# Feed-forward entries of a streaming encoder: six pairs of weight chunks as seven block products each, with the block sums made on GpSimd

## What is computed

```python
def pre_mod(h, g_pre, shift, scale):
    return rmsnorm(h, g_pre) * (1 + scale[:, None, :]) + shift[:, None, :]
def swiglu(x, w1, w2):
    g, u = jnp.split(x @ w1, 2, axis=-1)
    return (jax.nn.silu(g) * u) @ w2
...
for l in range(DEPTH):
    mp = adaln(c_prompt, w_ada[l], b_ada[l])
    ...
    hp = post_add(hp, swiglu(pre_mod(hp, g[0], mp[0], mp[1]), ffn_w1[l, 0], ffn_w2[l, 0]), g[1], mp[2], FFN_RES)
    ...
    hp = post_add(hp, swiglu(pre_mod(hp, g[4], mp[6], mp[7]), ffn_w1[l, 1], ffn_w2[l, 1]), g[5], mp[8], FFN_RES)
```

## Time and profile before

| | |
|---|---|
| median of 3 runs | 2681.08 us |
| the profiled execution | 2681.71 us, span 2679.8 us |
| PE, PEld busy | 2645.8, 2563.3 us |
| DVE, ACT, POOL busy | 1636.2, 963.1, 200.0 us |
| matmuls | 20698 |
| granted PE clock, mean | 0.997 |

### The profile page before, as it was taken

How to read it: one execution, slowest core, us unless ns; L and a number is a source line. 1 busy time by engine, 2 the same in 40 slices (tenths; PEclk the granted TensorE clock), 3 DMA queues, 4 the chain that set the end, 5 groups by cost and what they waited for, 6 DMA issues and landing times.

```text
span 2679.8 us, 49072 instructions
## 1 busy us (share of the span) xinstructions
PE 2645.8 (99%) x20698; PEld 2563.3 (96%) x20698; DVE 1636.2 (61%) x3542; ACT 963.1 (36%) x1792; POOL 200.0 (7%) x371
## 2 busy tenths in 40 slices
PE   7999999999999999999999999999999999999997
PEld 6999999888999999999999999998889999999997
DVE  4677666765555577776577776276655445555523
ACT  4232324444422442232252223255452336322321
POOL 0111010110000001111101111001100000000000
PEclk9999999999999999999999999999999999999998
DMA  6444453343333224445424444234332222333321
GB/s 261 126 146 141 157 177 113 124 130 109 95 111 111 87 95 154 136 144 168 131 89 152 139 159 161 88 98 141 119 105 80 87 83 76 99 109 105 95 82 65
DMA packets 92987, 324.79 MB, mean 121 GB/s; under 512 B 13980, under 2 KB 17628, under 8 KB 92064
## 3 DMA queue, kind: packets, MB, share of 16 engines
q1 hardware_dynamic: 62512, 221.72, 26.3%
q0 software_dynamic: 30256, 99.93, 11.2%
HBM read 310.70 MB, written 11.55 MB: 120 GB/s over the span
## 4 chain that ended last, share of the span: by engine, by line
PE 97%; DVE 1%; DMA 0%; issue 0%; ACT 0%; DVEq 0%; SPq 0%; ACTq 0%
PE ps L769 90%; PE ps L1131 2%; PE ps L1179 1%; PE ps L1155 1%; PE ps L778 1%; DMA ada_first<-in_ada_first 0%; PE ps L1148 0%; PE ps L823 0%; DVE prob L2242 0%; PE ps L909 0%; PE ps L1192 0%; DVE next L1792 0%; PE ps L807 0%; PE ps L832 0%; PE ps L1055 0%
## 5 line engine op out<-in xcount | busy, mean ns | idle before, releaser
L769 PE MATMUL ps<-x_hi,w_hi 128*128 128x288 f32 (+1 forms) x4224 | 938.9, 298 | 2.4 <-DVE x_lo L1883 1.5
L769 PE MATMUL ps<-x_lo,w_hi 128*128 128x288 f32 (+1 forms) x4224 | 922.5, 294 | 0.0
L769 PE MATMUL ps<-x_hi,w_lo 128*128 128x288 f32 (+1 forms) x4224 | 922.4, 294 | 0.0
L769 PEld LDWEIGHTS ps<-x_hi,w_hi 128*128 128x128 f32 x4224 | 682.6, 188 | 14.2 <-issue 8.0
L769 PEld LDWEIGHTS ps<-x_hi,w_lo 128*128 128x128 f32 x4224 | 685.7, 188 | 0.0
L769 PEld LDWEIGHTS ps<-x_lo,w_hi 128*128 128x128 f32 x4224 | 685.3, 188 | 0.3
L1715 DVE TENSOR_TENSOR w_lo<-w_raw,w_hi 128x1024 fp32r<-128x1024 f32 x384 | 468.1, 1222 | 160.1 <-ACT w_hi L1296 158.1
L1296 ACT CAST w_hi<-w_raw 128x1024 fp32r<-128x1024 f32 x384 | 391.9, 1048 | 72.4 <-DMA w_raw<-in_f 71.6
L769 PE MATMUL ps<-hid_hi,w_hi 128*128 128x288 f32 x1344 | 301.1, 295 | 0.0
L769 PE MATMUL ps<-hid_lo,w_hi 128*128 128x288 f32 x1344 | 299.3, 293 | 0.0
L769 PE MATMUL ps<-hid_hi,w_lo 128*128 128x288 f32 x1344 | 299.0, 294 | 0.0
(11 more groups left out here) (243 smaller groups left out, 2440.4 us busy)
## 6 DMA issues: line engine op xcount, KB each, us to landing
w_raw<-in_f SPq DMA_DIRECT2D x260, 512.0 KB, 3.7
ada_w<-in_ada POOLq DMA_DIRECT2D x256, 256.0 KB, 4.0
w_raw<-in_gate SPq DMA_DIRECT2D x64, 512.0 KB, 3.6
w_raw<-in_tri SPq DMA_DIRECT2D x40, 512.0 KB, 3.7
ada_first<-in_ada_first SPq DMA_DIRECT2D x4, 2048.0 KB, 21.0
w_raw<-in_wout SPq DMA_DIRECT2D x16, 512.0 KB, 3.6
c_half<-c_scratch POOLq DMA_DIRECT2D x11, 512.0 KB, 5.6
decay_p<-f_prompt POOLq DMA_DIRECT2D x8, 512.0 KB, 4.5
```

What stands on the lines that cost most here:

```text
L769: r = mm(ps[:, 2 * out + b, 0:width], w, xx[:, cols(b)], start=first and n == 0, stop=last and n == 2)
```

## The change

Pairs 7 to 12 of each entry (`JOIN0` to `JOIN1`-1), six of 21.5, become **joined pairs**. A pair is a product of a 2x2 block matrix of weights (g and u by the first and the last four feature blocks) with a 2x2 block matrix of x (first and last four feature blocks, first and last 288 tokens). It is made of seven block products instead of eight, each 4 tiles x 3 passes = 12 matmuls of 288 columns in a bank of its own (`join_bank`). For this:

- four sums of weight blocks per pair, 128x512 each, are added by POOL in place in the raw slots (`sum_of_w`). The loads bring each block to where it is needed, some twice, and the pair has four chunks, the last one a half (two, two, two and one products).
- four sums of x blocks (`t_raw`, 128x1152 each, once per entry) are added by POOL too (`t_sums`), and split by ACT and DVE.
- for that x has to be normalized: in pairs 1 and 2 DVE multiplies h by r2 and ACT applies scale and shift (`x_full`); in pair 4 (`NORMED`-1) the two chunks are interleaved by block (`chunk_pair`, in bank pairs 2 and 3), and behind the last reader of each block ACT and DVE write the halves of the normalized x in its place. From pair 5 on the products are of the normalized x, all 288 columns wide; DVE makes `hid` by one product of PSUM with Silu(g).
- DVE adds or subtracts the seven banks of a joined pair (`join_parts`, seven instructions of 288 columns).
- the `ada` units of the entries move to the joined pairs of the first entry (one each) and to pairs 13 to 20 (`f1_units`), and the tables of the other stages change with them. The number of units, 256, stays.

```diff
+JOIN0, JOIN1 = 7, 13
+JOINS = JOIN1 - JOIN0
+F1_CHUNKS = F1_LOADS + 2 * JOINS
...
-ADA_STAGES = [((0, "f1a"), (2, 4, 3)), ((0, "f2a"), (5, 7)), ((0, "gate"), (6,)), ((0, "f1b"), (8, 10, 9)),
-              ((0, "f2b"), (11, 13)), ((1, "f1a"), (12, 14, 15)), ((1, "f2a"), (16,)), ((1, "gate"), ()),
-              ((1, "f1b"), (17,)), ((1, "f2b"), ())]
-AFTER_PAIRS = ((0, "gate"), (1, "f1b"))
+ADA_STAGES = [((0, "f1a"), (2, 4, 3), (2, 4)), ((0, "f2a"), (3, 5, 7), (5, 7)), ((0, "gate"), (6,), (6,)),
+              ((0, "f1b"), (8, 10), (8, 10)), ((0, "f2b"), (9, 11), (9, 11)), ((1, "f1a"), (12, 13), (12, 13)),
+              ((1, "f2a"), (14, 16), (14, 16)), ((1, "gate"), (15,), (15,)), ((1, "f1b"), (17,), (17,)),
+              ((1, "f2b"), (), ())]
+AFTER_PAIRS = ((0, "gate"), (1, "gate"))
...
-    return 0 if i in (2, 11, KF - 2) else 1 if (l, ab) == (1, "b") else 3
+    if (l, ab) == (1, "b"):
+        return 2 if i >= JOIN1 else 0
+    if (l, ab) == (0, "a"):
+        return 1 if JOIN0 <= i < JOIN1 else {13: 5, 14: 5, 15: 6, 17: 5, 18: 5, 19: 4, 20: 4}.get(i, 0)
+    return {13: 5, 14: 5, 15: 6, 17: 4, 18: 4, 19: 4, 20: 4}.get(i, 0)
...
-    half = {(0, "a"): 8, (0, "b"): 8, (1, "a"): 4, (1, "b"): 0}[l, ab]
+    if (l, ab) == (0, "a"):
+        return iter([2, 3] * 4 + [2, 2, 0] + [2] * 8 + [0] * KF)
+    half = {(0, "a"): 8, (0, "b"): 8, (1, "a"): 8, (1, "b"): 0}[l, ab]
     return iter([2] * half + [0] + [2] * half + [0] * KF)
...
+        def load_joined(l, ab, i):
+
+            c = chunk(l, "f1" + ab, f1_chunk(i))
+            at = (2 * l + (ab == "b")) * F1_LOADS + 2 * i
+            g, u = ins["f1"][at:at + 1, :, :].rearrange("a p n -> (a p) n"), \
+                ins["f1"][at + 1:at + 2, :, :].rearrange("a p n -> (a p) n")
+            n = CHUNK_COLS // 2
+            loads = (None, ((n, u[:, n:2 * n]),), ((0, u[:, 0:n]), (n, g[:, n:2 * n])))
+            if i < JOIN1 - 1:
+                loads += (((n, ins["f1"][at + 2:at + 3, :, n:2 * n].rearrange("a p n -> (a p) n")),),)
...
+        def chunk_pair(l, ph, i, pairs, cols, ab):
+
+            c = chunk(l, ph, 2 * i)
+            chunk_ready(c)
+            chunk_ready(c + 1)
+            for k in range(KD):
+                for s in (0, 1):
+                    r = split_tile(pairs[s], c + s, k, x_hi[:, k, :], x_lo[:, k, :], cols, k == 0, k == KD - 1)
+                    if k == KD - 1:
+                        r.then_inc(chunk_done.sem, 1)
+                if k < KD - 1:
+                    r.then_inc(x_read.sem, 1)
...
+            if i == JOIN0:
+                pe.wait_ge(hid_ready.sem, hid_ready.done(l, (ab == "b") * (NORMED + 1) + NORMED - 1))
+            else:
+                pe.wait_ge(joined.sem, joined.done(l, 7 * (n - 1) + 4))
+            chunk_ready(c)
+            part(0, 0, 0, *x_block(0, 0)).then_inc(half_done.sem, 1)
+            t_wait(0)
+            part(1, 0, 1, *t_block(2)).then_inc(chunk_done.sem, 1)
+            chunk_ready(c + 1)
+            t_wait(1)
+            part(2, 1, 0, *t_block(1)).then_inc(half_done.sem, 1)
+            t_wait(2)
+            part(3, 1, 1, *t_block(3)).then_inc(chunk_done.sem, 1)
+            chunk_ready(c + 2)
+            t_wait(3)
+            if i == JOIN0:
+                pair_free(l, ph, 0, f1_group(0, JOIN1))
+            part(4, 2, 0, *t_block(0)).then_inc(half_done.sem, 1)
+            part(5, 2, 1, *x_block(half_k, 0)).then_inc(chunk_done.sem, 1)
+            chunk_ready(c + 3)
+            if i == JOIN0:
+                pair_free(l, ph, 1, f1_group(1, JOIN1))
+            else:
+                pe.wait_ge(joined.sem, joined.done(l, 7 * (n - 1) + 5))
+            part(6, 3, 0, *x_block(half_k, 1)).then_inc(chunk_done.sem, 1)
 
...
+            more = i + 1 < JOIN1
+            if i > JOIN0:
+                low_of_joined(l, ab, i, 2)
+                low_of_hid(l, ab, i - 1)
+            join_parts(l, ab, i, 0)
+            join_parts(l, ab, i, 1)
+            if i > JOIN0:
+                low_of_joined(l, ab, i, 3)
+            join_parts(l, ab, i, 2)
+            join_parts(l, ab, i, 3)
+            join_parts(l, ab, i, 4)
+            if more:
+                low_of_joined(l, ab, i + 1, 0)
+            else:
+                split_lo()
+            join_parts(l, ab, i, 5)
+            join_parts(l, ab, i, 6)
+            if more:
+                low_of_joined(l, ab, i + 1, 1)
+            else:
+                split_lo()
+            ada(l, "f1" + ab, f1_units(l, ab, i), ada_junk[:, :])
+            product_of_joined(l, ab, i)
+            if not more:
+                split_lo()
+                low_of_hid(l, ab, i)
+
         modulated = [0]
 
-        def ada(l, ph, n):
+        def ada(l, ph, n, junk=None):
...
+                else:
+                    for k in range(KD):
+                        low_of_full(l, ab, k)
+                        if k in (2, 5):
+                            split_lo()
+                    dve.wait_ge(chunk_done.sem, chunk_done.done(0, chunk(l, ph, 2 * i + 1)))
+                    take(sil[:, i, :], 2, 2 * (i % 2)).then_inc(g_scaled.sem, 1)
+                    take(hid[:, i, :], 3, 2 * (i % 2) + 1)
...
+                else:
+                    split_lo()
+                    ada(l, ph, f1_units(l, ab, i) // 2)
+                dve.wait_ge(chunk_done.sem, chunk_done.done(0, chunk(l, ph, f1_chunk(i) + 1)))
+                dve.wait_ge(acc_free[0].sem, acc_free[0].done(l, GROUP_AT[ph][0] + f1_group(0, i)))
+                V.tensor_tensor(two(hid[:, i, :]), pair[1], two(sil[:, i, :]), ALU.mult).then_inc(acc_free[1].sem, 1)
+                if i == JOIN0 - 1:
+                    low_of_joined(l, ab, JOIN0, 3)
+                elif i > NORMED:
+                    split_lo()
+                low_of_hid(l, ab, i)
+                if i >= JOIN1:
...
+            c, n, at = chunk(l, "f1" + ab, f1_chunk(i)), CHUNK_COLS // 2, 4 * joined_index(ab, i)
+            low, high = slice(0, n), slice(n, 2 * n)
+            g, u, more, last = ((c + v) % SLOTS for v in range(4))
+            if order == 0:
+                pool.wait_ge(raw_full[g].sem, raw_landed(c))
+                operands = w_in[:, g, high], w_in[:, g, high], w_in[:, g, low]
+            elif order == 1:
+                pool.wait_ge(w_sum.sem, w_sum.done(l, at))
+                pool.wait_ge(raw_full[u].sem, raw_landed(c + 1))
+                operands = w_in[:, u, low], w_in[:, g, high], w_in[:, u, high]
+            elif order == 2:
+                pool.wait_ge(w_sum.sem, w_sum.done(l, at + 1))
+                pool.wait_ge(chunk_done.sem, chunk_done.done(0, c + 3 - SLOTS))
+                spare = c + 2 if i == JOIN0 else c - 1
+                pool.wait_ge(raw_full[spare % SLOTS].sem, raw_landed(spare))
+                operands = w_in[:, last, low], w_in[:, u, low], w_in[:, spare % SLOTS, high]
+            else:
+                pool.wait_ge(raw_full[more].sem, raw_landed(c + 2))
+                operands = w_in[:, more, low], w_in[:, more, low], w_in[:, u, high]
+            nc.gpsimd.tensor_tensor(*operands, ALU.add).then_inc(w_sum.sem, 1)
+
...
+        def sums_and_loads(l, ab):
+            ph = "f1" + ab
+            ada_loads(l, ph, 0, 2)
+            at = 2
+            t_sums(l, ab)
+            for i in range(JOIN0, JOIN1):
+                if i > JOIN0 + 1 and f1_units(l, ab, i):
+                    ada_loads(l, ph, at, at + 1)
+                    at += 1
+                for order in range(4):
+                    sum_of_w(l, ab, i, order)
+            ada_loads(l, ph, at)
```

376 lines of the change are left out of this document (331 added, 45 removed).

## The result

The changed kernel takes 2658.0 us (median of 4 runs, 2657.0 to 2658.9), the kernel before 2681.3 in the same comparison: a ratio of 0.9913, 95% interval 0.9896 to 0.9930. So 23.3 us were won where fewer matmuls alone would have given 37.9. The profiled execution has a span of 2655.3 us, 24.5 less than before.

The account below looks back on a forecast made before the run. TensorE was taken as the bound, busy 2645.8 of 2679.8 us. From the profiled 2681.7 us, - 37.9 (matmuls) + 12 (ada units) + 0 = 2655.8; against the median 2655.2, rounded 2656; range 2643 to 2680.

Parts of the forecast that it names:

- The wait that was named as the sign of being right: Pair 16 of three entries: TensorE idle near 3.6 us, released by VectorE's product, with VectorE waiting for `ada_w`.
- the one named as the sign of being wrong: Inside the joined pairs: TensorE waiting for `w_lo` would show the forecast wrong.
- The matmuls, 37.9 us: Joined pairs of four entries: 288 matmuls fewer at 131.7 ns each, a gain of 37.9 us.
- Joined pairs, 0: Joined pairs: additions, weight halves and loads stay covered within 11.06 us a pair, so 0 us lost.
- The timetable: One joined pair, from TensorE's start: VectorE needs 8.8 of 11.06 us, 10.2 in the first entry; no wait while s under 1.70.
- the exclusion as a rival: Joined pairs: GpSimd's adds and VectorE's two-operand instructions exclude each other, 5.35 + 4s a pair; together 6 us, 2662; chance 0.25.
- s: Joined pairs: time of one GpSimd add of 128x512, taken as 1.22 us, bounds 0.6 and 2.44.
- x behind pair 4, 0: Pairs 1 to 4: normalizing and splitting x is covered by 4 us, so 0; lateness beyond that costs the excess, four times.
- The ada units, 12 us: Pairs 13 to 20: moved units delay VectorE's products; TensorE waits 3 x 3.6 + 1.1 = 12 us, ends 9 and 21.
- the reload of 4.7: Ada units: a buffer comes back after 4.5 to 5.2 us, taken as 4.7; with two buffers one unit per 3.0 us.
- First down projection and layer 1's mixer, 0: First down projection: a lag of 10 us just covered by 10.6, so 0, bound 3; layer 1's mixer: 16 units, 0.
- all cover holds: Rival on the ada units: with buffers back in under 3.9 us the 12 us vanish, 2643.2 us; chance 0.2.

Follow-up runs that it names:

- experiment 7: The changed kernel with GpSimd's load of ada_w behind the second of a joined pair's four additions instead of ahead of the first; 2657.2 us.
- 1: The kernel before with 24 additions of 128x512 on GpSimd, results unread, in the first of layer 0's entries b; 2689.9 us, ratio 1.0036.
- 2: The changed kernel with two of the four additions of each joined pair cut from 512 columns to 8; 2650.6 us, ratio 0.9888.
- 3: The changed kernel with each of GpSimd's 96 additions of weight blocks replaced by a copy of its second operand; 2649.8 us, ratio 0.9884.
- 4: The changed kernel with each of GpSimd's 96 additions of weight blocks replaced by setting the same columns to a constant; 2649.6 us (one run).
- experiment 5: The changed kernel with the first entry's six joined-pair ada units moved, two to pair 3, four to pairs 17 to 20; 2664.7 us, ratio 0.9938.
- 11: The changed kernel with 12 instead of 11 ada units between pair 13's end and pair 15's product, second and third entry; 2661.8 us, ratio 0.9931.
- experiment 6: The changed kernel with five of the first entry's six joined-pair ada units moved forward to pairs 1 to 3; 2654.5 us, ratio 0.9904.
- 8: The changed kernel with one weight half instead of two among VectorE's eight low halves of x in pair 4; 2658.5 us, ratio 0.9918.
- 9: The changed kernel with GpSimd's four combinations of x started only behind the last low half of x in pair 4; 2659.1 us, ratio 0.9918.
- 10: The changed kernel with later x combinations, two weight additions between them, and VectorE's pair 6 order t, t, w, w, t, t, w; 2654.6 us, ratio 0.9903.
- 12: The changed kernel with five ada units moved forward to pairs 1 to 3, later x combinations and reordered pair 6; 2647.5 us, ratio 0.9875.

## Why the prediction was right, and where not

The time, 2656, was right within 0.1%, and that is luck. Its terms were off on both sides and made up for each other: 12 us of lag that did not come, and 12 us (8.0 + 3.4 of exclusion, and 0.5 in the fourth entry, whose cause was not followed up) and 1.8 us of slower matmuls that the sum had at 0. The wait that was named as the sign of being right, near 3.6 us in pair 16 of three entries, was missing, and the one named as the sign of being wrong, for `w_lo` inside the joined pairs, was there.

- *The matmuls, 37.9 us.* Right in the main: 288 fewer. But six joined pairs without a wait take 66.8 us and not 66.4, since the matmuls on t_hi and t_lo come every 133.1 ns, so 36.1 us.
- *Joined pairs, 0.* Wrong for the first entry. The timetable had 10.2 of 11.06 us on VectorE, with GpSimd as if alone. I had the exclusion as a rival, its formula too, 5.35 + 4s, but with s = 1.22 it gave 0.5 us over in each of five pairs, 2.6 in all. Measured: s 1.28 to 1.31 alone, so 0.84 over, 4.2 in all; the stage lost 8.0. Two steps failed. The sum let GpSimd run as if alone. And the rival counted the shared time only as a sum, where the order of the steps decides. The timetable had begun the right chain (the slot free at 9.48, two additions, the `w_lo` of the second chunk) and stopped there. Followed through the unit, the product and the `w_lo` of the third chunk, with its own lengths, it ends at 9.48 + 0.2 + 2.44 + 1.14 + 1.35 + 0.68 + 1.14 = 16.4, where TensorE needs it at 11.06 + 6.32 = 17.4. That is 1 us to spare by the forecast lengths and 0.4 by the measured ones, and 2.3 us of stretching (experiment 7) are 1.9 too much in a pair. Experiments 1 to 5 show the exclusion and that the unit's 1.35 us is needed for the loss. For the other entries the rival said 3 us; measured at most 0.5, in the fourth alone.
- *s itself.* I took 1.22 between 0.6 and 2.44; alone it is 1.28 to 1.31. The estimate from the Trainium skill's figure (GPSIMD Engine Reference, section Elementwise) was 1.12, 0.17 too little.
- *x behind pair 4, 0.* Wrong in three entries, 1.1 us each. The condition was named (over 4 us late costs the excess), but I asked only how much work VectorE had there, not what GpSimd would do to it. The exclusion stood in a rival of the joined pairs and was never applied to the combinations, 11.5 us of GpSimd in one piece.
- *The ada units, 12 us.* Right in mechanism, wrong in size: TensorE did not wait there. The product of pair 15 was forecast 10.0 us behind its due time and ended 5.5 behind it, just inside the 6.3 us of the g chunk. The step that failed is the reload of 4.7. The second entry, pair 14 (a unit is 1.35 us from its start):

```profile
1104.31 0.76 DVE L2112 CUSTOM_DVE_ANT_0 ps<-ada_w,c_half,ada_all 128x512 f32<-128x512 f32 x1
...
1108.87 0.76 DVE L2112 CUSTOM_DVE_ANT_0 ps<-ada_w,c_half,ada_all 128x512 f32<-128x512 f32 x1 [1.79 <-DMA ada_w<-in_ada]
...
1131.87 0.75 DVE L2193 TENSOR_TENSOR hid<-ps,sil 128x576 f32<-128x576 f32 x1
```

The first unit ends at 1105.66 and its buffer is back at 1108.87, after 3.2 us; the six such gaps of these pairs have 3.1 to 4.8, mean 3.8. My rival put the edge at 3.9. The page's landing fell from 4.0 to 3.3. I had taken 4.7 from two gaps of the timeline, 4.49 and 5.16, which turned out to be long ones. By my own schedule 0.1 us of reload is about 0.4 us of wait, so that 3.8 leaves about none. Experiments 5 and 11 show that the mechanism holds as soon as a unit or a slower load is added.
- *First down projection and layer 1's mixer, 0.* Right: no wait. Experiment 5 shows how thin the cover of the first is: a unit more in each of pairs 19 and 20 and the lag behind them cost 4.2 us.

So the case that came is a mixture: the lag rival's "all cover holds" and the exclusion. I had priced them as alternatives; they are independent, and a sum of both, 2643.2 plus the exclusion, was the better frame: with the measured 12 + 1.8 it gives 2657.

## What to carry to other kernels

When work goes to a third engine, ask what it shares with the second: here GpSimd reading SBUF cost VectorE about its own length (1.15 to 1.45 us for an addition of 1.3) in the instructions with two SBUF operands that it met, and was held up itself. So the place of the work counts more than its amount: follow the chain through all engines until it closes on itself, with each step stretched that can meet the other engine, and compare it with a pair's time. Put it where VectorE reads PSUM or waits, and look for the loss in single durations of the timeline, not in means. Moving one step out of a stretched chain only moves the wait (8 and 9); a gain came when everything that was late next was moved too (10, 12).

## What was not expected of the hardware

- After an idle time of 4.0 us TensorE's granted clock was 0.50 for some 5 us of work (experiment 5, 274.5 to 279.7; it had fallen at about 273, still idle), and 2 us were lost on top of the wait; after one of 1.9 us it was 0.50 for some 3.4 us (experiment 6), from 97.0 on, 1.3 us after the work had begun again. Behind the waits of 0.5 and 1.0 us in the changed kernel it stayed at 1.00. So the 3.6 us waits that I had forecast would have cost more than 3.6 each; the sum did not have that.
- Beside VectorE, GpSimd's addition of 128x512 lasted up to 3162 ns against 1282 alone; its copy took 638 (median), a constant 527. The constant did not disturb VectorE's work in the joined pairs.
- VectorE's recorded duration holds the time in which it is shut out: no wait and no idle time appears for it. On the page only the means show it, and faintly for VectorE: `w_lo` 1250 ns instead of 1222, GpSimd's additions 1549 instead of 1282.
